# Weight sums of a seven-product quad made by accumulating DMA, 14 quads a layer, some of them in pairs, in a one-core encoder trunk

## What is computed

```python
for i in range(DEPTH):
    x = x + rmsnorm(hybrid_mixer(rmsnorm(x, g[0]), ...), g[1])
    x = x + rmsnorm(memory_xattn(rmsnorm(x, g[2]), ...), g[3])
    x = x + rmsnorm(conv_ffn(rmsnorm(x, g[4]), w_up[i], conv_w[i], conv_b[i], w_down[i]), g[5])

def conv_ffn(h, w_up, conv_w, conv_b, w_down):
    u = h @ w_up                       # 2048 -> 8192, then a causal convolution of width 3
    gate, val = jnp.split(c, 2, axis=-1)
    return (jax.nn.gelu(gate, approximate=True) * val) @ w_down   # 4096 -> 2048
```

## Time and profile before

| | |
|---|---|
| Median of 3 runs | 1967.22 us |
| Profiled execution | 1967.25 us, its span 1965.4 us |
| PE busy | 1953.2 us (99%) |
| DVE, ACT, POOL busy | 1506.8 us (77%), 1138.3 us (58%), 187.5 us (10%) |
| DMA | 393.94 MB, 200 GB/s in the mean |
| Granted TensorE clock | 0.999 of full speed |

### The profile page before, as it was taken

How to read it: one execution, slowest core, us unless ns; L and a number is a source line. 1 busy time by engine, 2 the same in 40 slices (tenths; PEclk the granted TensorE clock), 3 DMA queues, 4 the chain that set the end, 5 groups by cost and what they waited for, 6 DMA issues and landing times.

```text
span 1965.4 us, 30703 instructions
## 1 busy us (share of the span) xinstructions
PE 1953.2 (99%) x10639; PEld 1679.4 (85%) x10639; DVE 1506.8 (77%) x2326; ACT 1138.3 (58%) x1770; POOL 187.5 (10%) x212
## 2 busy tenths in 40 slices
...
GB/s 319 200 205 154 171 209 242 200 150 169 203 193 204 202 205 201 203 272 242 226 149 227 151 151 161 216 216 196 155 153 204 203 201 209 188 205 211 267 253 132
DMA packets 111490, 393.94 MB, mean 200 GB/s; under 512 B 13140, under 2 KB 14560, under 8 KB 110048
## 3 DMA queue, kind: packets, MB, share of 16 engines
...
...
HBM read 382.35 MB, written 10.24 MB: 200 GB/s over the span
## 4 chain that ended last, share of the span: by engine, by line
PE 97%; DVE 2%; ACT 1%; issue 0%; DVEq 0%; POOL 0%; ACTq 0%; POOLq 0%
PE ps L967 24%; PE ps L970 12%; PE ps L881 11%; PE ps L883 11%; PE ps L882 11%; PE ps L893 11%; PE ps L896 5%; PE ps L1278 2%; PE ps L1276 2%; PE ps L1277 2%; PE ps L845 1%; PE ps L1227 1%; DVE w_lo L1757 1%; PE ps L1215 0%; PE ps L1213 0%
## 5 line engine op out<-in xcount | busy, mean ns | idle before, releaser
L1757 DVE TENSOR_TENSOR w_lo<-raw,w_hi 128x1024 fp32r<-128x1024 f32 (+2 forms) x660 | 778.7, 1187 | 323.2 <-ACT w_hi L1333 316.8
L1333 ACT ACTIVATE w_hi<-raw 128x1024 fp32r<-128x1024 f32 (+2 forms) x660 | 671.9, 1028 | 343.8 <-PE ps L970 219.1
L967 PE MATMUL ps<-h_t,w_hi 128*128 128x512 f32 x2032 | 638.8, 396 | 0.0
L970 PEld LDWEIGHTS ps<-h_t,w_lo 128*128 128x128 f32 x2032 | 381.7, 188 | 90.2
L970 PE MATMUL ps<-h_t,w_lo 128*128 128x256 f32 x2032 | 399.2, 278 | 0.0
L967 PEld LDWEIGHTS ps<-h_t,w_hi 128*128 128x128 f32 x2032 | 309.3, 189 | 0.0
L893 PE MATMUL ps<-h_t,w_hi 128*128 128x512 f32 x768 | 246.8, 403 | 0.0
L896 PEld LDWEIGHTS ps<-h_t,w_lo 128*128 128x128 f32 x768 | 144.2, 188 | 33.9
L2501 POOL TENSOR_SCALAR up_c<-up_u,cw 128x256 f32<-128x256 f32 x128 | 130.3, 1030 | 369.8 <-DVE up_u L2335 369.8
L896 PE MATMUL ps<-h_t,w_lo 128*128 128x256 f32 x768 | 151.2, 278 | 0.0
L881 PE MATMUL ps<-w_hi,act_t 128*128 128x512 f32 x320 | 124.5, 389 | 0.0
...
## 6 DMA issues: line engine op xcount, KB each, us to landing
raw<-stream SPq DMA_DIRECT2D x640, 512.0 KB, 4.2
comb<-comb_hbm SPq DMA_DIRECT2D x24, 512.0 KB, 4.9
comb_hbm<-comb_out ACTq DMA_DIRECT2D x14, 512.0 KB, 6.1
...
x<-x_in SPq DMA_DIRECT2D x4, 512.0 KB, 13.3
```

Of the source, the lines that this page charges most:

```text
L967: pe.matmul(ps[:, 4 * half + nt, :], hi[:, cc, nt * P:(nt + 1) * P], h_t[:, c, :, :], start=(c == 0), stop=False, skip_group_check=True)
L970: mm = pe.matmul(ps[:, 4 * half + nt, SEQ:2 * SEQ], lo[:, cc, nt * P:(nt + 1) * P], h_t[:, c, 0, :], start=False, stop=(c == KC - 1), skip ...
L1333: act.activation(w_hi[:, slot, 0:width], raw[:, rslot, 0:width], ACT.Copy).then_inc(hi_ready, 1)
L1757: dve.tensor_tensor(w_lo[:, slot, 0:width], raw[:, rslot, 0:width], w_hi[:, slot, 0:width].bitcast(F32), ALU.subtract).then_inc(lo_ready, 1)
```

## The change

1. `SEVEN` has seven values in place of six, so 14 quads a layer in place of 12. The order of a pass is new: in pass 0 it is N5, quad 0, N7, quads 2 and 4, N9, quads 6 and 8, N11, quad 10, N13, quad 12; in pass 1 quad 0, N5, quads 2 and 4, N7, quads 6 and 8, N9, quad 10, N11, quad 12 (the numbers are j). So two quads stand in a row twice a pass. Counted through a layer, the quads are n = 0 to 13; the pairs are n = (1, 2), (3, 4), (8, 9) and (10, 11).
2. `first_sums` is gone from DVE. Two transfers on POOL's queue take its place: a plain one brings `ra.first` and `rb.first` from HBM into `sums[0:2]`, POOL waits until it has landed (`b_put`), and an accumulating one (`accum_op=ALU.add`) adds `rb.first` and `rb.second` to them from HBM (`b_got`). ACT's slot B and DVE's `other_sums` wait for `b_got`.
3. There are two buffers of sums, used in turn. Quad n may be loaded once DVE has finished slot C of quad n - 2; quads 0 and 1 once PE is through with the up projection; the quads 8, 10 and 12 also wait for the merges of pass 0.
4. For a pair, the `other_sums` of both quads are made ahead of the first quad's slot A. For slot D, SP loads only the second half of rb into `raw`.

```diff
-SEVEN = [0, 2, 4, 6, 8, 10]
-PASS_HEAD, PASS_TAIL = [1, 3], [[14, 15], [12, 14, 15]]
-PASS_MID = [[5, 0, 7, 2, 9, 4, 11, 6, 13, 8, 12, 10], [0, 5, 2, 7, 4, 9, 6, 11, 8, 13, 10]]
+SEVEN = [0, 2, 4, 6, 8, 10, 12]
+PASS_HEAD, PASS_TAIL = [1, 3], [[14, 15], [13, 14, 15]]
+PASS_MID = [[5, 0, 7, 2, 4, 9, 6, 8, 11, 10, 13, 12], [0, 5, 2, 4, 7, 6, 8, 9, 10, 11, 12]]
...
-        psum_b = sb("psum_b", [P, 4, 512], 88 * K)
+        psum_b = [sb(f"psum_b{i}", [P, 4, 512], at) for i, at in enumerate((88 * K, 104 * K))]
...
+        def first_sums(l, n):
+
+            m = l * len(SEVEN_AT) + n
+            return b_got[n % 2], 16 * (m // 2 + 1)
...
                     sp.wait_ge(lo_ready, raw_done(l, p - RAW))
-                    sp.dma_start(raw[:, p % RAW, :], stream[l * NPIECES + p]).then_inc(landed[p % RAW], 16)
+                    c = 512 if P_DOWN + DOWN_FREED[p - P_DOWN] - 1 in SEVEN_AT else 0
+                    sp.dma_start(raw[:, p % RAW, c:], stream[l * NPIECES + p][:, c:]).then_inc(landed[p % RAW], 16)
...
-                        act.wait_ge(b_sums, 3 * n + (1 if kind == "B" else 3))
+                        if kind == "B":
+                            act.wait_ge(*first_sums(l, n - l * len(SEVEN_AT)))
+                        else:
+                            act.wait_ge(b_sums, 2 * n + 2)
...
-                def first_sums(s):
...
-                    dve.wait_ge(*raw_landed(l, ra))
-                    dve.wait_ge(*raw_landed(l, rb))
-                    dve.tensor_tensor(psum_b[:, 0:2, :], raw[:, ra % RAW:rb % RAW + 1, 0:512],
-                                      raw[:, rb % RAW, :].rearrange("p (a n) -> p a n", n=512), ALU.add).then_inc(b_sums, 1)
...
+                def other_sums(s):
 
                     ra, rb = [(P_DOWN + DOWN_SPLITS[s - P_DOWN + d][4]) for d in range(2)]
...
+                    if n > 1:
+                        dve.wait_ge(lo_ready, l * NSPLITS + SEVEN_AT[n - 2] + 4)
+                    dve.wait_ge(*first_sums(l, n))
+                    dve.wait_ge(*raw_landed(l, rb))
+                    dve.tensor_tensor(sums[:, 2, :], sums[:, 0, :], raw[:, rb % RAW, 512:1024], ALU.add).then_inc(b_sums, 1)
+                    dve.wait_ge(b_sums, m + 1)
                     dve.wait_ge(*raw_landed(l, ra))
...
+                    dve.tensor_tensor(sums[:, 3, :], sums[:, 2, :], raw[:, ra % RAW, 512:1024], ALU.add).then_inc(b_sums, 1)
...
-                    if s + 2 in SEVEN_AT:
-                        first_sums(s + 2)
-                    if s + 1 in SEVEN_AT:
+                    if s + 1 in SEVEN_AT and s - 3 not in SEVEN_AT:
                         other_sums(s + 1)
+                        if s + 5 in SEVEN_AT:
+                            other_sums(s + 5)
...
+                for n, s in enumerate(SEVEN_AT):
+                    p = l * NPIECES + P_DOWN + DOWN_SPLITS[s - P_DOWN][4]
+                    if n < 2:
+                        pool.wait_ge(*pieces_used(l, P_DOWN))
+                    else:
+                        pool.wait_ge(lo_ready, l * NSPLITS + SEVEN_AT[n - 2] + 4)
+                    if DOWN_SPLITS[s - P_DOWN][1] == 1 and n % 2 == 0:
+                        pool.wait_ge(odd_merged, 2 * l + 1)
+                        pool.wait_ge(even_merged, 2 * l + 1)
+                    _, got = first_sums(l, n)
+                    pool.dma_start(psum_b[n % 2][:, 0:2, :], stream[p:p + 2, :, 0:512].rearrange("a p n -> p a n")).then_inc(b_put[n % 2], 16)
+                    pool.wait_ge(b_put[n % 2], got)
+                    pool.dma_start(psum_b[n % 2][:, 0:2, :], stream[p + 1].rearrange("p (a n) -> p a n", n=512),
+                                   accum_op=ALU.add).then_inc(b_got[n % 2], 16)
```

More of the change, by code:

```diff
@@ L662, in build @@
         b_sums = sem("b_sums")
+        b_put = [sem(f"b_put{i}") for i in range(2)]
+        b_got = [sem(f"b_got{i}") for i in range(2)]
         m1_copied = sem("m1_copied")
@@ L1920, in other_sums @@
-                def other_sums(s):
-                    ra, rb = [(P_DOWN + DOWN_SPLITS[s - P_DOWN + d][4]) % RAW for d in range(2)]
-                    n = 3 * (l * len(SEVEN_AT) + seven(s))
-                    dve.wait_ge(b_sums, n + 1)
-                    dve.tensor_tensor(psum_b[:, 2, :], psum_b[:, 0, :], raw[:, rb, 512:1024], ALU.add).then_inc(b_sums, 1)
-                    dve.wait_ge(b_sums, n + 2)
-                    dve.tensor_tensor(psum_b[:, 3, :], psum_b[:, 2, :], raw[:, ra, 512:1024], ALU.add).then_inc(b_sums, 1)
+                    m = 2 * (l * len(SEVEN_AT) + n)
@@ new lines, in other_sums @@
+                    sums = psum_b[n % 2]
+                    if n > 1:
[4 more added lines that the diff above has]
+                    dve.wait_ge(b_sums, m + 1)
+                    dve.wait_ge(*raw_landed(l, ra))
+                    dve.tensor_tensor(sums[:, 3, :], sums[:, 2, :], raw[:, ra % RAW, 512:1024], ALU.add).then_inc(b_sums, 1)
```

18 lines of the change are left out of this document (7 added, 11 removed).

## The result

| | before | after |
|---|---|---|
| Median | 1967.22 us (1967.09 to 1967.56, 6 runs) | 2097.70 us (2091.37 to 2102.84, 6 runs) |
| Ratio | | 1.0663, 95% interval 1.0652 to 1.0674 |
| Profiled execution | 1967.25 us, span 1965.4 us | 2093.48 us, span 2091.7 us |
| Granted TensorE clock, mean | 0.999 | 0.974 |

In the changed kernel's lines the quads' matmuls are L1284 to L1286, DVE's split of `raw` is L1768, its split of sums L1915, `other_sums` L1928 and L1931, POOL's load L2519 and accumulating transfer L2521.

A forecast was written before the change was run, and what follows sets the result against it. PE's matmuls were taken to bound the down projection; stalls of 49.1 us a layer, 98.2 in all, less 2.7 for 12 matmuls saved, gave +95.5 us: 2063 us, range 1998 to 2120.

The forecast's parts named there:

- Removing `first_sums` from DVE: Taking 24 instructions of 1.22 us, 29 us, off DVE gains 0, since PE does not wait for DVE.
- `comb` and the two more quads: Down projection: later `comb` loads on SP's queue and four more split slots a layer on DVE each cost 0.
- Quad 0: First quad of a layer: transfers stand behind POOL's last up convolution, so PE waits 13.1 us for slot A.
- W: POOL's permission to DVE's go: load L 5.4, accumulating transfer A 6.7, releases 0.4; 12.5 us, bounds 6.6 and 16.6.
- Quads 1 and 2: First pair: quad 2's load waits for quad 0's slot C, and PE stalls 7.4 us ahead of quad 1.
- Quads 3 and 4, 10 and 11: Pairs behind a pair: first quad's load must land before the second's is issued; PE stalls 8.0 us each.
- Quads 5 and 12: Single quads behind a pair: the two transfers outlast PE's work, a stall of 2.6 us each.
- The upper bound: Load and accumulating transfer both at 8.1 us, taken as POOL's slowest bulk load: W 16.6, +163.7 us, 2131.
- Short transfers: Rival: POOL's load and accumulating transfer as short as SP's, 3.1 to 4.1 us, giving 1991 to 2011; chance 0.15.
- An accumulating transfer slower than any load: Rival: accumulating transfers take over 9.5 us, each us more costing 14 in all, so over 2102; chance 0.14.
- The clock: Rival: PE returns from long stalls at 1.2 GHz, adding 17 us at pairs, 2080; chance 0.10 for over half.
- A faster kernel: Rival: the transfers are hidden, no sum is late, and 12 fewer matmuls give 1964.5 us; chance 0.03.

The follow-up runs named there:

- Kernel 1: The changed kernel with the first sums made by DVE again and each quad's `other_sums` right ahead of its own slot A: 1970.69 us, ratio 1.0018.
- Kernels 7: As Kernel 1, with the quads spread apart so that five pairs in a row a layer are left: 1969.03 us, ratio 1.0010.
- kernel 9: First sums on DVE, quads spread apart, and in a pair the second quad's half sums made behind its slot A: 1968.15 us, ratio 1.0005.
- 12: Quads spread apart, first sums on DVE except those of each pair's second quad, which GpSimd computes without a transfer: 1978.15 us, ratio 1.0057.
- kernel 2: The changed kernel with each quad's second transfer a plain copy in place of an accumulating one: 2063.3 us, ratio 1.0495.
- kernel 8: The changed kernel with 37 to 54 matmuls on zeros ahead of slot A of quads 0, 1, 3, 8 and 10: 2106.68 us, ratio 1.0706.
- (5): The changed kernel with each quad's `other_sums` right ahead of its own slot A, also in pairs: 2045.1 us, ratio 1.0391.
- (11): The changed kernel without the loads of the sum buffers from the third quad of a layer on: 2020.73 us, ratio 1.0273.
- (4): The changed kernel with quad 0's transfers and quad 1's load issued ahead of POOL's last convolution: 2091.79 us, ratio 1.0631.

## Why the prediction was right, step by step

**The mechanism.** It went as written: PE stands ahead of slot A, DVE ahead of it in `other_sums`, POOL's two transfers in a row ahead of that. Kernel 1 shows it: with the sums on DVE 4.0 of the 100.3 us of waits are left. The forecast of 2063 us was 31 to 35 us short, inside its range. Of what the profile was to show, the waits ahead of slot A and DVE's waits for the transfer came; that the longest stands at quad 0 and that those of the pairs are about equal did not (13.3 at a quad 3, 4.7 at a quad 1).

**Removing `first_sums` from DVE: 0.** Right as far as it goes: DVE fell to 1493.4 us and nothing came of it. Kernels 7, 9 and 12 add that DVE is not free everywhere: over two quads in a row it is late by tenths of a microsecond if it makes the first sums.

**`comb` and the two more quads: 0.** Right. No wait of PE on `comb` or on `raw` is listed.

**Quad 0: W + 0.6 = 13.1.** It was 8.9. POOL's convolution took 3.95 us, not 5.96, now that DVE's sums no longer ran beside it, and permission came 1.9 us sooner; and W was 10.1, with A = 5.1, while SP's queue was silent.

**Quads 1 and 2: W - 5.1 = 7.4.** 9.3. The arithmetic of the chain holds (3.0 to permission, 13.8, 2.6 to slot A: 19.4 of the 19.49 us from quad 0 to quad 1); W was 1.3 larger (A 9.5 for 6.7, L 4.0 for 5.4), and permission 0.4 later by the clock.

**Quads 3 and 4, 10 and 11: 8.0 each.** 13.0 and 12.1, the step that failed most. I took the way over quad 3's load for the longer one. The way over quad 2's release was: at 1.2 GHz PE left quad 1 some 2.3 us later, permission came after 10.0 us and not 7.4, and then came W = 17.0, because the load of quad 4 ran beside quad 3's accumulating transfer and SP's stream and took 11.0. The forecast gave one L and one A to all transfers; they share the DMA engines, which these four and the stream fill.

**Quads 5 and 12: 2.6 each.** 2.5 and 2.6 in layer 0, but not as waits: these are the slower matmuls behind the waits at quads 3 and 10, so the number was right there by another cause. In layer 1 the waits came, 2.04 and 2.09. Quads 6 and 13, forecast 0, gave 1.6 and 2.7 in layer 0, 0.5 and 1.0 in layer 1.

**The sum.** 49.1 a layer against 60.9 and 61.5. These 24 us, and the 6.5 by which kernel 1's span lies over that of the 12 matmuls saved (1969.2 against 1962.7), are the 30.8 us between the forecast and the profiled execution. That PE's listed waits of layer 0 also add up to 49.1 is chance: too much at quad 0 stands against too little at the pairs.

**The upper bound.** It rests on a wrong reading. The transfers of 7.5 to 8.1 us in the earlier trace rows are no bulk loads; the list of DMA issues of the kernel before has them with 6 KB:

```profile
f_q<-f_hbm POOLq DMA_DIRECT2D x2, 6.0 KB, 7.8
```

The slowest bulk load of that queue was `f_k`'s of 7.9, and W passed the bound of 16.6 in the changed kernel, up to 18.1 us at quad 4 of layer 1.

**The rivals.** Short transfers: half true, a load alone lands in 4.0 to 4.1, but not the second one. An accumulating transfer slower than any load: it costs 1.4 us more than a plain one at quad 0, where SP's queue is silent, and 34 us over the kernel (kernel 2); A over 9.5 for all was wrong. The clock: the fall to 1.2 GHz behind waits is there (0.50), as the Trainium skill ("TensorE: Matmul & The Clock Gate", Part 1) has it, and 28 us of PE's busy time are its mark. It also bore on the path: the 2.3 us at quads 3 and 4. But kernel 8, with the clock held behind eight of ten waits, did not get faster, and DMA was full in the stretch behind quad 1. Its price in a kernel whose DMA has room was not measured, and in some places of kernel 8 the zero matmuls may themselves have held PE up. A faster kernel: kernel 9 comes within 0.05% of before, none lies below it.

**Shares of the 130 us.** 53 us came from making a pair's sums together (5), 77 from the loads (11), 34 from adding (2). They overlap, and must not be added up. For the place behind the convolution (4) no share is shown.
